# Reordering VectorE and ScalarE steps inside the attention jobs of a hybrid decoder step on one core

## The reference, cut to what matters

```python
# differential attention, 4 heads: two softmax maps per head
a = probs(q1, k1) - lam * probs(q2, k2)          # masked, float32
out_a = a @ v                                     # 128-wide values
# forgetting attention, 8 heads, run here as 4 pairs
s = q @ k.T * scale + C[t] - C[s]                 # C: running sum of log gates
out_f = softmax(s) @ v                            # 64-wide values
# samples: the same two attentions over the cached pages and the new row
```

## Time and profile before

| | us |
|---|---|
| median of 3 runs | 1421.01 |
| lowest and highest run | 1420.81, 1422.69 |
| the profiled execution | 1416.69 |
| its span | 1414.9 |
| TensorE busy in the span | 1383.2 |
| VectorE, ScalarE, GpSimd busy | 924.9, 629.9, 505.4 |

### The profile page before, as it was taken

The page is one execution under the profiler, slowest core; times in us unless marked ns, Lnnn a source line. Parts: engine busy times, 40 slices in busy tenths (PEclk is TensorE's granted clock), DMA queues, the critical chain, the costliest instruction groups (busy, mean ns, idle before and its releaser), DMA issues. The chain is left out here.

```text
span 1414.9 us, 27711 instructions
## 1 busy us (share of the span) xinstructions
PE 1383.2 (98%) x10564; PEld 1246.5 (88%) x10564; DVE 924.9 (65%) x1513; ACT 629.9 (45%) x1216; POOL 505.4 (36%) x715
## 2 busy tenths in 40 slices
PE   7999999999999999999999999999999999999998
PEld 6999877877777677577899999999999999999998
DVE  6421776676676776675549967766766666655685
ACT  7743655554454554543334523332333243434552
POOL 4213768755566551021101343344324421000052
PEclk9999999999999999999999999999999999999999
DMA  6113557778767663632322354454445437656683
GB/s 195 46 50 92 171 159 223 222 245 249 242 198 221 218 214 101 209 121 76 105 84 66 108 163 149 145 166 149 142 135 171 147 121 261 194 161 201 207 264 105
DMA packets 219390, 229.78 MB, mean 162 GB/s; under 512 B 24739, under 2 KB 151531, under 8 KB 219220
## 3 DMA queue, kind: packets, MB, share of 16 engines
q1 hardware_dynamic: 219258, 228.01, 51.7%
HBM read 181.06 MB, written 46.99 MB: 161 GB/s over the span
## 5 line engine op out<-in xcount | busy, mean ns | idle before, releaser
L644 POOL TENSOR_TENSOR k_page<-k_page,q_bc 128x256 f32<-128x256 f32 x256 | 187.2, 762 | 134.7 <-DMA k_page<-in_cache_fox_k 97.5
L1282 PE MATMUL PS<-ht_hi,w_hi 128*128 128x344 f32 x576 | 193.8, 337 | 2.6 <-DVE ht_lo L955 1.4
L1282 PE MATMUL PS<-ht_hi,w_lo 128*128 128x344 f32 x576 | 184.6, 320 | 0.0
L1282 PE MATMUL PS<-ht_lo,w_hi 128*128 128x344 f32 x576 | 184.3, 320 | 0.0
L2774 PE MATMUL PS<-act_hi,wd_hi 128*128 128x258 f32 x616 | 139.8, 285 | 1.2 <-DVE acc L2592 0.6
L862 ACT ACTIVATE probs<-probs,stat 128x256 f32<-128x256 f32 (+7 forms) x128 | 98.5, 771 | 93.1 <-DVE stat L1126 92.7
L2774 PE MATMUL PS<-act_hi,wd_lo 128*128 128x258 f32 x616 | 138.5, 283 | 0.0
L2774 PE MATMUL PS<-act_lo,wd_hi 128*128 128x258 f32 x616 | 138.3, 283 | 0.0
L1282 PEld LDWEIGHTS PS<-ht_hi,w_hi 128*128 128x128 f32 x576 | 109.0, 189 | 27.5 <-issue 20.3
L2722 PE MATMUL PS<-ht_hi,wgu_hi 128*128 128x258 f32 x608 | 122.6, 283 | 0.0
L2722 PE MATMUL PS<-ht_hi,wgu_lo 128*128 128x258 f32 x608 | 122.5, 283 | 0.0
(11 more groups left out here) (311 smaller groups left out, 3349.8 us busy)
## 6 DMA issues: line engine op xcount, KB each, us to landing
b_dram<-conv SPq DMA_DIRECT2D x77, 258.0 KB, 3.1
k_page<-in_cache_diff_k SPq DMA_DIRECT2D x64, 256.0 KB, 2.9
k_page<-in_cache_fox_k SPq DMA_DIRECT2D x64, 256.0 KB, 3.3
v_page<-in_cache_diff_v SPq DMA_DIRECT2D x64, 256.0 KB, 2.8
v_page<-in_cache_fox_v SPq DMA_DIRECT2D x64, 256.0 KB, 3.2
act_raw<-b_dram SPq DMA_DIRECT2D x55, 258.0 KB, 2.8
w_raw<-in_w_in SPq DMA_DIRECT2D x24, 512.0 KB, 5.0
wgu_raw<-in_w_gate SPq DMA_DIRECT2D x22, 512.0 KB, 4.3
```

The lines of the kernel that those rows point to most:

```text
L644: ins = pool.tensor_tensor(kpage[:, g % 2, c:c + PIECE], kpage[:, g % 2, c:c + PIECE], qbc[:, c:c + PIECE], ALU.mult)
L1282: ins = pe.matmul(PS[:, z_bank(c), 0:THIRD], b[:, k, :], a[:, k, third(i)], start=(k == 0 and p == 0), stop=(k == KC - 1 and p == 2))
```

## The change

Five edits, all of order; no instruction is added or removed, and no operand, buffer or semaphore changes.

1. VectorE, jobs 1 to 32: `weights(J-1)` moves from behind maximum 1 to ahead of maximum 0.
2. VectorE, units 4 to 6, tiles 6 and 7: the copy of a_t of J-2 moves ahead of maximum 0.
3. VectorE, tile 0 of units 5 and 6: the copy of a_t moves ahead of the page work (sum of a key page, page maxima).
4. ScalarE, tile 2 of units 0 to 6: the copy of the samples' rows moves ahead of both exponentials.
5. ScalarE, units 4 to 6, tiles 6 and 7: the copy of the weighted sum of J-2 moves between the two exponentials. `exponentials(J)` is split into `exponential(J, m)` for this.

```diff
--- before.py
+++ after.py
@@ -855,12 +855,11 @@
                     act.wait_ge(x_done, X[e] + 1)
                     act.activation(at[:, m, c:c + nblk, :], bank_of(e)[:, 0:nblk * P].rearrange("p (k q) -> p k q", q=P), ACT.Copy).then_inc(act_evac, 1)
 
-            def exponentials(J):
-                for m in range(2):
-                    act.wait_ge(max_done, 2 * J + m + 1)
-                    p = probs[:, 2 * (J % 2) + m, 0:(tile(J) + 1) * P]
-                    act.activation(p, p, ACT.Exp, bias=stat[:, J % 8, m:m + 1], scale=-1.0,
-                                   accum_out=stat[:, J % 8, 2 + m:3 + m]).then_inc(exp_done, 1)
+            def exponential(J, m):
+                act.wait_ge(max_done, 2 * J + m + 1)
+                p = probs[:, 2 * (J % 2) + m, 0:(tile(J) + 1) * P]
+                act.activation(p, p, ACT.Exp, bias=stat[:, J % 8, m:m + 1], scale=-1.0,
+                               accum_out=stat[:, J % 8, 2 + m:3 + m]).then_inc(exp_done, 1)
 
             def sums_out(J):
                 e = ("o", J)
@@ -910,20 +909,28 @@
                 n = {1: k_tile(u + 1) + 1, 5: k_tile(u + 2)}.get(t, len(TILES))
                 if n < len(TILES):
                     split_hi(n)
+                between = J < LAST_UNIT and t >= 6 and fox(J - 2)
                 if J < LAST_UNIT:
-                    exponentials(J)
+                    if t == 2:
+                        rows(("s", u))
+                    exponential(J, 0)
+                    if between:
+                        sums_out(J - 2)
+                    exponential(J, 1)
                     chunks(before)
                 if J >= LAST_UNIT:
                     chunks(before)
                 if J < NJ:
                     for e in rows_at(J):
-                        rows(e)
-                if J >= 2 and fox(J - 2):
+                        if e[0] != "s" or J >= LAST_UNIT:
+                            rows(e)
+                if J >= 2 and fox(J - 2) and not between:
                     sums_out(J - 2)
                 if LAST_UNIT <= J <= NJ:
                     turned(J - 1)
                 if LAST_UNIT <= J < NJ:
-                    exponentials(J)
+                    exponential(J, 0)
+                    exponential(J, 1)
                 if J in turn_jobs:
                     turned_hi(*turn_jobs[J])
                 chunks(after)
@@ -1161,12 +1168,17 @@
 
             behind_first = [4 * NT + NT - 1, 5 * NT + NT - 1, 6 * NT + NT - 1]
             for J in range(NJ + 3):
+                if 1 <= J <= LAST_UNIT and not fox(J - 1):
+                    weights(J - 1)
+                turned_first = J >= LAST_UNIT or tile(J) >= 6
+                if 2 <= J < NJ + 2 and fox(J - 2) and turned_first:
+                    turned(J - 2)
                 if J < LAST_UNIT:
                     maximum(J, 0)
+                if 2 <= J < NJ + 2 and fox(J - 2) and not turned_first:
+                    turned(J - 2)
                 if J - 1 in behind_first and J < LAST_UNIT:
                     pages_and_norms(J - 1)
-                if 2 <= J < NJ + 2 and fox(J - 2):
-                    turned(J - 2)
                 if LAST_UNIT <= J <= NJ:
                     scaled(J - 1, 0)
                 if LAST_UNIT <= J < NJ:
@@ -1180,8 +1192,6 @@
                 elif 1 <= J < LAST_UNIT and fox(J - 1):
                     scaled(J - 1, 0)
                     scaled(J - 1, 1)
-                elif 1 <= J < LAST_UNIT:
-                    weights(J - 1)
                 if 2 <= J < NJ + 2 and not fox(J - 2):
                     rows_out(J - 2)
                 for g in k_pages(J - 2):
```

## The result

The changed kernel takes 1426.47 us (median of 20 runs, 1421.62 to 1431.40); the kernel before, timed beside it, takes 1418.84 (20 runs, 1416.11 to 1422.69). The ratio is 1.0053, with a 95% interval of 1.0043 to 1.0063: **7.5 us slower**. The forecast was 2.0 us slower, 1423.0, with a range of 1416.5 to 1427.0. The range holds the time, but only by luck: it was built on 1421.01, the median of 3 runs of before, and 20 runs put before at 1418.84. Counted from before, the range was 4.5 us faster to 6.0 slower, and 7.5 lies outside it. The loss is nearly four times what the sum gave, so the question is what the sum left out.

The account below looks back on a forecast made before the run. TensorE was taken as the bound. Units 0 to 3 gave 4.2 + 1.0 - 2.8 = +2.4 us, the others 0, a GpSimd wait -0.4: +2.0 on 1421.0 makes 1423.0 us, range 1416.5 to 1427.

Parts of the forecast that it names:

- What bounds the kernel: TensorE is the bound, busy 223.7 of 229.0 us in units 0 to 3; each us won or lost reaches the end.
- Edit 1, cost in tile 4: Units 0 to 3: weights delay maxima, exponentials and key rows, so TensorE waits; +4.2 us, bounds 2.0 and 4.9.
- the 0.3 of slack given to it: Tile 4 of unit 3 shows no key-row wait, so 0.3 us was estimated as slack and taken off 4.5.
- Edit 1, cost in tiles 0, 1 and 3: Rows behind exponentials come 1.25 to 1.7 us later, but half a chunk covers them; +1.0 us, bounds 0 and 3.
- the third rival: Taken up elsewhere: waits for transfers and GpSimd, fixed in time, swallow TensorE's loss; change 0, 1421 us; chance 0.20.
- Edit 1, the gain: Units 0 to 3: earlier weights end TensorE's waits for merged maps, sample rows and some q_t; 2.8 us, bounds 1.6 and 4.1.
- Edit 4: Tile 2: sample rows first win 0.9 us in unit 0; later exponentials cost +0.4 in unit 6, bounds 0 and 1.
- Edit 3: Start of unit 6: TensorE's 1.20 us wait for a_t goes, a later wait keeps some; -0.9 us, bounds -1.2 and -0.4.
- Edit 2: Units 4 to 6, tiles 6 and 7: VectorE must now wait for TensorE's transposes; +0.9 us in sum, bounds 0 and 2.
- Edit 5: Units 4 to 6, tiles 6 and 7: costed jointly with the early a_t copies there, +0.9 and -0.4 us, no separate size.
- The 0.4 us taken up by the wait for GpSimd (L655): A TensorE wait of 0.4 us for GpSimd's pages, which hang on transfers, takes up some delay; -0.4 us.
- The second rival, a merged map held up by GpSimd: Units 0 to 3: GpSimd holds up L1099 ahead of the maxima, 0.4 us more per tile; +6, 1427 us; chance 0.17.

Follow-up runs that it names:

- tile4_only: The kernel before with VectorE's weights ahead of both maxima in tile 4 of units 0 to 3 only; ratio to before 1.0025, +3.5 us.
- undo_edit2: The changed kernel with a_t in tiles 6 and 7 of units 4 to 6 again behind maximum 0; ratio to before 1.0039, +5.5 us.
- chosen: Kernel before plus weights ahead in tiles 2, 5, 6, 7 (units 0 to 3), a_t ahead of page sum, sample rows ahead of exponentials; ratio 0.9984, -2.3 us.
- samples_only: The kernel before with only ScalarE's sample rows copied ahead of the exponentials in tile 2; ratio to before 0.9989, -1.6 us.
- fox_only: Kernel before plus only the changes in units 4 to 7: a_t ahead of maximum 0 and page sum, weighted sums between exponentials; ratio 1.0007, +1.0 us.
- one_copy_early: The kernel before with a_t copied ahead of maximum 0 in one job only, the last tile of unit 4; ratio to before 1.0008, +1.1 us.
- rows_ahead: Kernel before with weights ahead of both maxima, and key and value rows of tiles 0, 1, 3, 4 copied ahead of exponentials; ratio 1.0000, 0.0 us.
- weights_only: The kernel before with only VectorE's weights of units 0 to 3 moved ahead of both maxima; ratio to before 1.0043, +6.1 us.
- no_edit2: Kernel before with a_t ahead of the page sum and weighted sums between exponentials, a_t of tiles 6 and 7 left behind maximum 0; ratio 0.9987, -1.8 us.

## Why the prediction came out as it did

**What bounds the kernel: right.** TensorE stayed the bound, and what was lost in units 0 to 3 reached the end whole.

**Edit 1, cost in tile 4: right in mechanism and size.** The sum said 4.2 us. In after TensorE falls back in tile 4 by 1.20, 1.08, 1.16 and 0.94 us, 4.4 in all; in the runs tile4_only has 3.5. The waits came to the 1.0 to 1.5 us that the prediction named. Unit 3 lost 0.2 us less than the mean of the other three, near the 0.3 of slack given to it. There was no idle time of VectorE left ahead of the maxima: by form, those at 128x640 now show none, against 0.7, as the sum assumed.

**Edit 1, cost in tiles 0, 1 and 3: the first term that was mis-sized.** The sum had 1.0, with a bound of 3. After falls back by 0.87, 0.34 and 0.58 us in tile 0 of units 2 to 4 and waits 0.60 us for key rows in tile 3 of unit 0: 1.8 up to the start of unit 4, 2.4 with it. The step that failed is "half a chunk of 12 matmuls stands between them and the ring entry". It does, but it covers little. In tile 0 of unit 2 in before, the copy ends 0.7 us ahead of that entry; in after the weights hold the maxima back by 1.69 us (260.57 to 262.26), the upper end of the 1.25 to 1.7 of the prediction, and TensorE waits 0.67 us. First the copy and the entry in before, then the entry in after:

```profile
258.85 0.57 ACT L850 ACTIVATE v_rows<-PS 128x512 f32<-128x512 f32 x1
...
260.12 0.38 PE L1407 MATMUL PS<-ident,probs 128*128 128x128 f32 x2
```

```profile
264.10 0.41 PE L1417 MATMUL PS<-ident,probs 128*128 128x128 f32 x2 [0.67 <-ACT v_rows L850]
```

**Two losses that no term held.** Tile 3 of unit 0 is 1.75 us longer in all, 1.15 more than its wait for key rows; 0.75 of that is a wait for z_raw (L748). This wait stands in that job in after, undo_edit2 and chosen alone, the three profiles that won 0.8 to 1.1 us in the job ahead of it, and chosen has it without edit 1 in tile 3. So the gain in tile 2 of unit 0, which the sum counted at 0.9, was given back one job later, much as in the third rival. And tile 3 of unit 3 lost 0.59 us to a wait for GpSimd's `w_lo` (L617). That one isn't the edit's as far as the profiles show: the same wait is 0.71 in samples_only, 1.08 in fox_only and 1.76 in one_copy_early, which have no edit 1.

**Edit 1, the gain: mechanism right, rather too high.** The sum had 2.8; unit 0 (tile 2 and tiles 6 and 7), the ends of units 1 and 2 and tiles 5 to 7 of unit 3 gave 3.7, less 0.4 lost in tile 5 of unit 0. But the 0.8 of tile 2 was given back, and 0.4 of what tiles 5 and 6 of unit 3 gave stands in the profiles without edit 1 too. About 2.1 are the edit's. All the steps together, 4.4 + 1.8 + 1.15 + 0.6 - 3.4, are the 4.5 us of units 0 to 3.

**Edit 4: right sign.** Forecast -0.9 in unit 0 and +0.4 in unit 6; measured -1.6 alone, and unit 6 does not pay.

**Edit 3: right mechanism, too small.** Forecast -0.9, measured -2.4 alone and 2.3 us in the profiled job. The sum let VectorE's page sum take some of it back as a later wait. The wait that stood there before, 0.68 us for VectorE's scores behind the sum, went as well.

**Edit 2: the second failure.** The sum costed it at +0.9 by counting waits. The waits came out at less than that in unit 4 (0.2 us), and the price was paid in the clock, of which the prediction only says that it is 1.00. It took TensorE's full clock for a constant of the stretch, and so put the clock at nothing in its sum; in after it cost 4.3 us of the trace, 2.6 of them in the job that edit 2 changes. By the ratios, edits 3 and 5 without edit 2 are 2.8 us faster than with it, and the changed kernel 2.0.

**Edit 5:** not shown either way; 0.9987 with it and 0.9983 without are the same.

**The 0.4 us taken up by the wait for GpSimd (L655): not seen.** That wait is 0.6 us in after, against 0.4.

**The second rival, a merged map held up by GpSimd: partly there.** L1106 at 128x512 has a mean of 1.009 us, against 0.800: 0.2 us in each of four tiles and not the 0.4 of that rival, and not the 1.2 us from which it would have decided. But its mechanism decided elsewhere, in tile 3 of unit 6. Before and after:

```profile
513.86 1.14 DVE L1144 SCALAR_TENSOR_TENSOR q_t<-q_t,head_stat,g_sub 128x128 f32<-128x128 f32 x4
```

```profile
520.07 3.03 DVE L1151 SCALAR_TENSOR_TENSOR q_t<-q_t,head_stat,g_sub 128x128 f32<-128x128 f32 x4
...
519.22 2.26 POOL L617 TENSOR_TENSOR w_lo<-w_raw,w_hi 128x256 fp32r<-128x256 f32 x3
521.44 2.27 POOL L644 TENSOR_TENSOR k_page<-k_page,q_bc 128x256 f32<-128x256 f32 x3
```

The same four norms take 3.03 us in place of 1.14, 0.76 each, exactly as long as one GpSimd piece (2.27/3), and GpSimd works without a gap beside them; before, it stood still from 513.1 to 515.4. These 1.9 us are about what TensorE waits in the next tile, 0.59 and 1.08 us. The Trainium skill (SBUF — State Buffer, Who interferes with whom) has the rule: a VectorE instruction with two SBUF inputs and a GpSimd instruction that reads SBUF lock each other out for a whole instruction, and whichever starts first goes first. The trace agrees, one piece of 0.76 us for each. No edit touches these lines; how the shifted job falls together with GpSimd's pieces decides. After comes to it 4.4 us later than before and rows_ahead, without edit 4, 2.5 later: both have the 3.03 us and the waits (0.87 and 1.08 us in rows_ahead). Weights_only comes 5.4 us later, undo_edit2 8.3, and there the four norms stay at 1.1 us and cost nothing.

## What to carry to other kernels

A step moved ahead on one engine is paid by whatever the next engine does behind the step that it delays: here ScalarE's copies stood behind the exponentials, and moving those copies into its idle time took the loss away (+6.1 us to 0.0). Give each such follower its cover in us against the delay at its longest form, not its mean.

Where TensorE is the bound, count not only how long it waits in a stretch but how its waits lie. Here, taking away one of two waits that had the same slow engine behind them did not shorten them: it joined them or moved them together, and in the profile the joined wait cost 2.6 us in clock and 0.2 in waiting. Over many executions the mean granted clock tells such a cost; one profile does not.

## What the hardware showed that I had not expected

The 14 profiles hold 13 falls of TensorE's clock between the start of unit 0 and the last microseconds. Each comes inside a wait of TensorE or within 1 us behind it: single waits of 1.40, 1.65, 1.68, 1.71 and 2.81 us, two of 2.35 and 2.10 us with one of 0.68 close behind, and pairs of 0.59 and 1.08, 1.02 and 0.62, and 1.38 and 1.26. The clock then stays at 1.2 GHz for 3.4 us (11 falls) or 6.8 (2 falls), although TensorE has work most of that time: from about 432.5 to 439.4 and from 528.1 to 531.5 in after. Where I compared the same matmuls in before, the 3.4 us cost 1.3 to 1.7 us of TensorE's time and the 6.8 us 2.6 to 2.8.

It does not follow from the waits alone. The last job of unit 7 has the same two waits, 1.38 and 1.26 us, in all 14 profiles. In ten of them the clock stays up, in four (no_edit2, undo_edit2, tile4_only, chosen) it falls. Before, and then no_edit2, where the granted clock of 600 to 604 is 0.74 and the same 28 matmuls take 3.06 us in place of 1.75:

```profile
600.45 0.98 PE L1407 MATMUL PS<-ident,probs 128*128 128x128 f32 x7 [1.38 <-DVE probs L1109]
602.69 1.75 PE L1420 MATMUL PS<-a_t,v_rows 128*64 128x128 f32 x28 [1.26 <-DVE a_t L1133]
```

```profile
600.32 0.98 PE L1411 MATMUL PS<-ident,probs 128*128 128x128 f32 x7 [1.38 <-DVE probs L1113]
602.57 3.06 PE L1424 MATMUL PS<-a_t,v_rows 128*64 128x128 f32 x28 [1.26 <-DVE a_t L1137]
```

Nor does a longer wait always bring it. In tile4_only the clock is 1.00 on both sides of a wait of 2.44 us, longer than all but one of those above, and in undo_edit2 behind one of 1.80; in rows_ahead it is 1.00 behind the pair of 0.87 and 1.08 in tile 3 of unit 6, where 0.59 and 1.08 brought it down in after.

```profile
234.90 0.27 PE L1442 MATMUL PS<-ident,page_max 128*16 128x128 f32 x1 [2.44 <-ACT k_rows L850]
```

In samples_only a transfer did it: a value page came late in unit 7, TensorE waited 2.35 us, and from tile 5 to tile 7 that kernel fell 4.4 us further behind before.

```profile
588.65 0.61 PE L1469 MATMUL PS<-v_page,scores 128*4 128x256 f32 x8 [2.35 <-DMA v_page<-in_cache_fox_v]
...
590.00:592.00 2.00, 2.00 (x15) 1.07 (x15) 0.24 (x2) 0.00 (x0) 0.00 (x0) 0.50 0.74 201
```

The falls also go with the differences between runs of one kernel: in weights_only a run with a clock of 0.999 took 1421.9 us and that with the lowest (0.993) 1431.2. What makes one wait tip the clock and another not isn't settled by these runs.
